# Experts stage: activations turned two chunks at a time, placing next to the turns of gathered rows, Silu on ScalarE

## The reference, cut to what matters

```python
def expert_block(args):
    xb, e = args
    u = xb @ w1[e] + b1[e]
    glu = jnp.minimum(u[:, ::2], SWIGLU_LIMIT)
    lin = jnp.clip(u[:, 1::2], -SWIGLU_LIMIT, SWIGLU_LIMIT)
    a = glu * jax.nn.sigmoid(SWIGLU_ALPHA * glu) * (lin + 1.0)
    return a @ w2[e] + b2[e]
```

## Time and profile before

| | us |
|---|---|
| median of the runs | 3635.84 |
| the profiled execution, device time | 3630.8 |
| its span, from the first to the last instruction | 3629.0 |
| units of experts, 790.5 to 2034.7 of the span | 1244 |

### The profile page before, as it was taken

One profiled execution on the slowest core, in us unless ns is written; L12 is line 12 of the kernel. 1 busy time (PEld: TensorE's weight loads), 2 busy tenths in 40 slices (PEclk: granted clock), 3 DMA queues, 4 the chain that ended last, 5 costly groups with the idle time before them and its releaser, 6 DMA issues. The chain is left out here.

```text
span 3629.0 us, 55793 instructions
## 1 busy us (share of the span) xinstructions
PE 3391.6 (93%) x20926; PEld 2738.5 (75%) x20926; DVE 2085.2 (57%) x2480; ACT 1764.9 (49%) x2318; POOL 1051.8 (29%) x435
## 2 busy tenths in 40 slices
PE   7989999989999999999999698899999987789997
PEld 4877777668888888888888584678887856678886
DVE  3320121279999999999999625521153155346665
ACT  3222333257777777777777524432243243133333
POOL 1324222212323232323232240144443300034443
PEclk9999999989999999999999899999999978899999
DMA  8213343359999999999999627123222300013221
GB/s 280 85 59 99 118 137 123 102 192 383 365 382 365 384 362 384 363 383 363 382 363 382 237 77 267 66 90 96 93 93 71 103 32 4 7 59 103 94 93 41
DMA packets 245253, 696.82 MB, mean 192 GB/s; under 512 B 17742, under 2 KB 149570, under 8 KB 186484
## 3 DMA queue, kind: packets, MB, share of 16 engines
q1 hardware_dynamic: 234932, 658.42, 48.9%
q0 software_dynamic: 9936, 36.18, 3.8%
q10 hardware_dynamic: 240, 0.12, 0.0%
HBM read 668.90 MB, written 30.23 MB: 193 GB/s over the span
## 5 line engine op out<-in xcount | busy, mean ns | idle before, releaser
L325 POOL TENSOR_TENSOR split_w<-ring,split_w 128x1024 fp32r<-128x1024 f32 (+1 forms) x294 | 698.2, 2375 | 1618.0 <-ACT split_w L320 1464.8
L2177 DVE TENSOR_TENSOR moe_low<-ring,moe_high 128x2048 fp32r<-128x2048 f32 x408 | 929.4, 2285 | 18.4 <-ACT moe_high L2167 17.4
L2167 ACT ACTIVATE moe_high<-ring 128x1024 fp32r<-128x1024 f32 x810 | 827.6, 1058 | 102.9 <-PE psum L2421 102.8
L320 ACT ACTIVATE split_w<-ring 128x1024 fp32r<-128x1024 f32 (+1 forms) x294 | 304.7, 1037 | 1030.6 <-PE psum L496 600.8
L2417 PE MATMUL psum<-moe_high,moe_xe 128*128 128x512 f32 x2176 | 585.6, 391 | 0.0
L2417 PEld LDWEIGHTS psum<-moe_high,moe_xe 128*128 128x128 f32 x2176 | 410.3, 189 | 83.6
L2328 POOL DMA_INDIRECT moe_y_rows<-moe_ye,moe_target x34 | 197.4, 5807 | 684.3 <-DVE moe_ye L2232 684.3
L496 PE MATMUL psum<-pair,split_w 128*128 128x512 f32 x1488 | 337.9, 389 | 0.0
L2421 PE MATMUL psum<-moe_low,moe_xe 128*128 128x512 f32 x1088 | 336.4, 391 | 0.0
L496 PE MATMUL psum<-b_pair,split_w 128*128 128x512 f32 x1392 | 321.8, 393 | 5.8 <-PEq L1406 2.6
L496 PEld LDWEIGHTS psum<-pair,split_w 128*128 128x128 f32 x1488 | 279.3, 188 | 58.7 <-issue 0.9
(11 more groups left out here) (640 smaller groups left out, 4342.7 us busy)
## 6 DMA issues: line engine op xcount, KB each, us to landing
ring<-in_w_experts SPq DMA_DIRECT2D x408, 1024.0 KB, 7.5
ring<-in_w_mod SPq DMA_DIRECT2D x48, 1024.0 KB, 6.7
ring<-in_w_in SPq DMA_DIRECT2D x39, 1024.0 KB, 5.2
ring<-in_w_up SPq DMA_DIRECT2D x33, 1024.0 KB, 5.1
ring<-in_w_in SPq DMA_DIRECT2D x44, 512.0 KB, 5.2
ring<-in_w_down SPq DMA_DIRECT2D x20, 1024.0 KB, 5.1
ring<-in_w_gate SPq DMA_DIRECT2D x11, 1024.0 KB, 5.3
ring<-in_w_out SPq DMA_DIRECT2D x8, 1024.0 KB, 6.5
```

Of the source, the lines that this page charges most:

```text
L320: self.nc.scalar.activation(high, raw, ACT.Copy).then_inc(self.K.rounded, 1)
L325: self.nc.gpsimd.tensor_tensor(low, raw, high.bitcast(F32), ALU.subtract).then_inc(self.K.split, 1)
L2167: self.nc.scalar.activation(self.B["high"][:, j % HALVES, :], self.raw(j), ACT.Copy).then_inc(self.high, 1)
L2177: self.nc.vector.tensor_tensor(flat(self.low_of(j, 2)), self.K.ring[:, self.ring_slot(j // 2), :], high, ALU.subtract).then_inc(self.low, 2)
```

## The change

Five things change, all in the experts' units.

- Activations are turned in two groups of four transposes instead of four groups of two. turn(0) takes chunks 0 and 1 and stands after half 9, in the middle of chunk 2; turn(1) takes chunks 2 and 3 and stands behind half 17. ScalarE's copy and VectorE's low part become two instructions of 128x512 each instead of four of 128x256.
- `pe_place` moves from behind chunk 0 to behind half 17, ahead of `pe_x_turn`, and works for the unit after the next. It also waits for `esel`, and a first placing stands before the loop.
- ScalarE computes Silu of 1.702 times the gate part instead of the sigmoid; one of VectorE's two multiplies per chunk (L2257) goes, and the factor 1/1.702 is put into the gates by one multiply of 128x1024 before the stage.
- The slots' base is subtracted by VectorE in `dve_stage` instead of being added by a matmul (L2388); two copies that prepared its operands go.
- On VectorE `dve_stage` moves ahead of low(8), `dve_pick` between clamp(1) and low(12), `dve_esel` between clamp(3) and multiply(3); on ScalarE the high parts are grouped anew around the gates and copies.

```diff
@@ class Experts, dve_unit @@
-        def low_of_turned(c):
-            ve.wait_ge(self.aT_high, u * 4 + (c + 1))
+        def low_of_turned(g):
+            ve.wait_ge(self.aT_high, u * 2 + (g + 1))
...
         def multiply(c):
-            ve.wait_ge(self.sig, u * 4 + (c + 1))
-            ve.wait_ge(self.clamped, u * 8 + (2 * c + 1))
-            nc.vector.scalar_tensor_tensor(B["glu"][:, c % 2, :], B["sig"][:, c % 2, :], SIG_LIMIT, B["lin"][:, c % 2, :],
-                                           ALU.min, ALU.mult).then_inc(self.clamped, 1)
-            ve.wait_ge(self.clamped, u * 8 + (2 * c + 2))
-            nc.vector.scalar_tensor_tensor(B["a"][:, c % 2, :], self.K.ps[:, c % 2, 0:256], LIMIT, B["glu"][:, c % 2, :],
+            ve.wait_ge(self.glu, u * 4 + (c + 1))
+            ve.wait_ge(self.clamped, u * 4 + (c + 1))
+            nc.vector.scalar_tensor_tensor(B["a"][:, c % 2, :], B["glu"][:, c % 2, :], GLU_LIMIT, B["lin"][:, c % 2, :],
                                            ALU.min, ALU.mult).then_inc(self.act_done, 1)
         low(6)
         clamp(0)
+        if ahead:
+            self.dve_stage(ve, u + 1)
         low(8)
         multiply(0)
-        if ahead:
-            self.dve_stage(ve, u + 1)
         low(10)
         clamp(1)
+        if ahead:
+            self.dve_pick(ve, u + 2)
         low(12)
         multiply(1)
+        low(14)
         low_of_turned(0)
-        low(14)
         clamp(2)
         low(16)
         multiply(2)
-        low_of_turned(1)
         low(18)
         clamp(3)
-        low(20)
-        multiply(3)
-        low_of_turned(2)
-        low(22)
         if ahead:
             self.dve_esel(ve, u + 1)
-        low_of_turned(3)
+        multiply(3)
+        low(20)
+        low_of_turned(1)
+        low(22)
         low(24)
...
@@ act_unit @@
-        nc.scalar.activation(B["unused"], self.K.ones[:, 0:1], ACT.Sigmoid)
+        nc.scalar.activation(B["unused"], self.K.ones[:, 0:1], ACT.Silu)
         high(6, 7, 8, 9)
-        sigmoid(0)
+        gate(0)
         high(10, 11, 12, 13)
-        sigmoid(1)
+        gate(1)
+        high(14, 15)
         turned(0)
-        high(14, 15, 16, 17)
-        sigmoid(2)
+        high(16, 17)
+        gate(2)
+        high(18, 19)
+        gate(3)
+        high(20, 21)
         turned(1)
-        high(18, 19, 20, 21)
-        sigmoid(3)
-        turned(2)
         high(22, 23, 24)
-        turned(3)
         if ahead:
             self.act_xe(sc, u + 1)
         high(25, 26, 27, 28, 29)
@@ pe_place, pe_unit @@
         if not first:
             pe.wait_ge(self.staged, v)
-        nc.tensor.matmul(out, B["eye"][:, :], B["slot_base"][:, :], start=True, stop=False)
+            pe.wait_ge(self.esel, v)
...
-        def turn(c):
-            pe.wait_ge(self.act_done, u * 4 + (c + 5))
-            pe.wait_ge(self.aT, u * 4 + (c + 4))
-            for i in range(2):
+        def turn(g):
+            pe.wait_ge(self.act_done, u * 4 + (2 * g + 6))
+            pe.wait_ge(self.aT, u * 2 + (g + 2))
+            for i in range(4):
...
             for i in range(4):
                 product(ps[:, c % 2, :], B["xe"], 4 * c + i, 2 * i, True)
-            if c:
-                turn(c - 1)
-            if c == 0 and ahead:
-                self.pe_place(pe, u + 1)
+                if (c, i) == (2, 1):
+                    turn(0)
...
             product(ps[:, 6 + m, :], B["aT"], j, 2 * k, False)
-            if j == 17 and ahead:
-                self.pe_x_turn(pe, u + 1)
-            if j == 18:
-                turn(3)
+            if j == 17:
+                if ahead:
+                    self.pe_place(pe, u + 2)
+                    self.pe_x_turn(pe, u + 1)
+                turn(1)
@@ mixture, TensorE before the loop @@
                 X.pe_x_turn(pe, 0)
+                X.pe_place(pe, 1)
                 pe.wait_ge(y_started, NT)
                 with pe.Fori(0, n1) as u:
                     X.pe_unit(pe, u)
```

More of the change, by code:

```diff
@@ L1924, in dve_step @@
             ve.wait_ge(self.b2_high, 1)
+            nc.vector.tensor_scalar(self.gates, self.gates, 1.0 / ALPHA, None, ALU.mult)
             nc.vector.tensor_tensor(self.b2[64:96, :], self.b2_raw[64:96, :], self.b2[64:96, :].bitcast(F32),
@@ L2129 @@
 LIMIT, ALPHA = 7.0, 1.702
-SIG_LIMIT = 1.0 / (1.0 + math.exp(-ALPHA * LIMIT))
+GLU_LIMIT = ALPHA * LIMIT / (1.0 + math.exp(-ALPHA * LIMIT))
 class Experts:
@@ L2143, in __init__ @@
         self.x_turned, self.xe_high, self.xe = n_("x_turned"), n_("xe_high"), n_("xe")
-        self.clamped, self.sig, self.act_done = n_("clamped"), n_("sig"), n_("act_done")
+        self.clamped, self.glu, self.act_done = n_("clamped"), n_("glu"), n_("act_done")
         self.kept, self.aimed, self.retired = n_("kept"), n_("aimed"), n_("retired")
@@ L2210, in dve_stage @@
             ve.wait_ge(self.kept, v)
-        nc.vector.tensor_scalar(B["source"][:, :], B["ps_place"][:, 0:1], -1.0, None, ALU.mult)
+        nc.vector.scalar_tensor_tensor(B["source"][:, :], B["ps_place"][:, 0:1], -1.0, B["slot_base"], ALU.mult,
+                                       ALU.subtract)
         nc.vector.tensor_reduce(B["gate_u"][:, bass.ds(v, 1)], B["ps_place"][:, 2:4], AX, ALU.add)\
@@ L2240, in low @@
             self.split(self.dve_low, ve, u, js, ahead)
-        def low_of_turned(c):
-            ve.wait_ge(self.aT_high, u * 4 + (c + 1))
-            out = B["aT"][:, :, 2 * c:2 * c + 2, :]
-            nc.vector.tensor_tensor(out[:, 1, :, :].rearrange("p a b -> p (a b)"), self.K.ps[:, 3, 0:256],
+        def low_of_turned(g):
+            ve.wait_ge(self.aT_high, u * 2 + (g + 1))
+            out = B["aT"][:, :, 4 * g:4 * g + 4, :]
+            nc.vector.tensor_tensor(out[:, 1, :, :].rearrange("p a b -> p (a b)"), self.K.ps[:, 3, :],
                                     out[:, 0, :, :].rearrange("p a b -> p (a b)").bitcast(F32), ALU.subtract)\
@@ L2293, in dve_unit @@
         self.dve_y(ve, u, 1)
-        if ahead:
-            self.dve_pick(ve, u + 2)
         low(28)
@@ L2349, in high, with gate, turned @@
             self.split(self.act_high, sc, u, js, ahead)
-        def sigmoid(c):
-            sc.wait_ge(self.clamped, u * 8 + (2 * c + 1))
+        def gate(c):
+            sc.wait_ge(self.clamped, u * 4 + (c + 1))
             sc.wait_ge(self.act_done, u * 4 + (c + 3))
[L2354 to L2360, removed]
-        nc.scalar.activation(B["unused"], self.K.ones[:, 0:1], ACT.Sigmoid)
+            nc.scalar.activation(B["glu"][:, c % 2, :], self.K.ps[:, c % 2, 0:256], ACT.Silu, scale=ALPHA)\
+                .then_inc(self.glu, 1)
+        def turned(g):
+            sc.wait_ge(self.a_turned, u * 2 + (g + 3))
+            nc.scalar.activation(B["aT"][:, 0, 4 * g:4 * g + 4, :].rearrange("p a b -> p (a b)"),
+                                 self.K.ps[:, 3, :], ACT.Copy).then_inc(self.aT_high, 1)
+        nc.scalar.activation(B["unused"], self.K.ones[:, 0:1], ACT.Silu)
         high(6, 7, 8, 9)
-        sigmoid(0)
+        gate(0)
         high(10, 11, 12, 13)
-        sigmoid(1)
+        gate(1)
+        high(14, 15)
         turned(0)
-        high(14, 15, 16, 17)
-        sigmoid(2)
+        high(16, 17)
[3 more added lines that the diff above has]
+        high(20, 21)
         turned(1)
-        high(18, 19, 20, 21)
-        sigmoid(3)
-        turned(2)
         high(22, 23, 24)
-        turned(3)
         if ahead:
@@ L2387, in pe_place @@
             pe.wait_ge(self.staged, v)
-        nc.tensor.matmul(out, B["eye"][:, :], B["slot_base"][:, :], start=True, stop=False)
+            pe.wait_ge(self.esel, v)
         for t in range(NT):
-            ins = nc.tensor.matmul(out, B["pick"][:, t, :], B["gcol"][:, t, :], start=False, stop=(t == NT - 1))
+            ins = nc.tensor.matmul(out, B["pick"][:, t, :], B["gcol"][:, t, :], start=(t == 0), stop=(t == NT - 1))
         ins.then_inc(self.placed, 1)
@@ L2438, in pe_unit @@
                 pe.wait_ge(self.y_ready, u * 2 + (m + 1))
-            if m == 0:
-                pe.wait_ge(self.aT, u * 4 + (k + 5))
+            if m == 0 and k % 2 == 0:
+                pe.wait_ge(self.aT, u * 2 + (k // 2 + 3))
             product(ps[:, 6 + m, :], B["aT"], j, 2 * k, False)
-            if j == 17 and ahead:
-                self.pe_x_turn(pe, u + 1)
-            if j == 18:
-                turn(3)
+            if j == 17:
[3 more added lines that the diff above has]
+                turn(1)
 def expert_source(A, e, chunk):
@@ L2469, in __init__ @@
              "h_rows": rows[0], "y_rows": rows[1], "iota": R.iota[:, :],
-             "sig": lane(4), "glu": lane(5), "lin": lane(6), "a": lane(7),
-             "b1": R.b1, "eye": R.eye, "slot_base": R.slot_base, "unused": R.slots[:, 7:8],
+             "glu": lane(5), "lin": lane(6), "a": lane(7),
+             "b1": R.b1, "slot_base": R.slots[:, 0:1], "unused": R.slots[:, 7:8],
              "gate_u": sb("gate_u", [P, EXPERTS + SPILLS + 1]), "gcol": R.gcol,
@@ L2544, in _ @@
```

(5 more changed lines are left out.)

5 lines of the change are left out of this document (1 added, 4 removed).

## The result

The changed kernel takes 3793.37 us, the median of four runs (3789.92 to 3795.84); the kernel before, beside it, 3635.78 us (3631.22 to 3636.49). The ratio is 1.043, with a 95% interval of 1.041 to 1.044: 158 us slower. The forecast was 3791.

What follows compares the result with a forecast made beforehand. The prediction took TensorE as the bound before, at 36.5 us a unit, and a loop of waits plus half clock after, at 41.0: 33 x (41.0 - 36.5) + 5.7 + 1 = 155 us on 3635.8 gives 3791, range 3728 to 3815.

Steps and rivals of the forecast that it cites:

- The bound and the gain: TensorE in each unit: 35.9 us if nothing waits, 0.6 less than before, 20 us over 33 units.
- Stretch (a): VectorE from the end of dve_xe_low to multiply(1), with 0.14 until TensorE starts: 17.0 us.
- Pause before turn(0): TensorE wants multiply(1) after half 9, before VectorE has it, and waits 2.5 us in each unit.
- (b): TensorE from the start of turn(0) to the end of turn(1): 13.4 us without the clock's cost.
- (c): From the end of turn(1) through ScalarE and VectorE to the end of dve_xe_low: 9.1 us; TensorE waits 1.0.
- The clock: Behind each turn(0), 3.4 us at half clock, costing 1.0 to 1.7 us a unit, taken as 1.5.
- clock holds: Rival in the units: the waits come as worked out but no half clock; 3742 us, chance 0.22.
- Start: Before unit 0, the first placing waits for dve_pick(1): beginning 5.7 us later, bounded by 3 and 6.
- Outside the stage: The multiply of the gates and two dropped copies, outside the units: between -0.4 and +1.2 us, taken as 0.
- The faster rival: In the units, multiply(1) comes before TensorE reaches turn(0), and TensorE's 35.9 us bounds: 3620 us, chance 0.06.

Runs made afterwards that it cites:

- e10: e7 with dve_stage moved behind multiply(0) on VectorE; 3619.6 us, ratio 0.996.
- e6: Changed kernel with all its parts, turn(0) still behind half 9, and new orders on VectorE and ScalarE; 3624.4 us, ratio 0.997.
- e8: Changed kernel with dve_pick behind multiply(1) instead of ahead of low(12); 3707.7 us.
- e4: Changed kernel with VectorE's order alone changed: multiply(1) directly behind clamp(1), low(12) and dve_pick later; 3661.6 us.
- e9: Changed kernel with the sigmoid and both multiplies back and the gates unscaled; 3809.0 us.
- e3: Changed kernel with ScalarE making high(22) and high(23) ahead of the copy turned(1); 3733.8 us.
- e7: Changed kernel with all its parts, turn(0) behind half 10, and other new orders on VectorE and ScalarE than e6; 3660.4 us.
- e2: Changed kernel with turn(0) one product later, behind half 10; 3691.8 us.

## Why the prediction was right

- **The bound and the gain.** TensorE's own work was worked out as 35.9 us a unit; the kernels without waits measured 35.98 and 36.02 (e10, e6). The gain was there, 0.5 us a unit; the order spent it. It was not the 20 us forecast, though: e6 and e10 lie 12 and 16 us under before, since they begin the stage 2 us later and their units gain 0.5, not 0.6.
- **Stretch (a), VectorE from the rows' low part to multiply(1).** 17.0 us worked out, 16.98 read off. That the pick's move doesn't count held: e8 takes it out of the stretch and gains its 0.86. That the stretch sets the unit is shown from both sides, by e4 (multiply earlier) and e9 (0.9 us longer, units without half clock 40.36 against 39.43 in the changed kernel's second unit).
- **Pause before turn(0).** 2.5 us worked out, 2.15 in the trace. Half of the difference is a matter of measure: the busy time of a matmul in the trace reaches beyond the start of the next one, 0.39 against steps of 0.23, and I had set the wait by the steps; by the steps it is 2.33. The rest is TensorE's way to turn(0), which took 14.65 us and not 14.5.
- **Stretch (b) and (c).** 13.4 + 1.5 for the clock against 14.87, and 9.1 against 9.11. ScalarE's copy ahead of the high parts cost 0.8 as a visible pause before the bias (1.0 was forecast, by the steps), and e3, which swaps them, gains 0.96.
- **The clock.** One stretch in each unit was taken, at 1.5 us; there were 31 in 33, at 1.54 (e3). The rival "clock holds" had 39.5 us a unit, and the changed kernel's second unit, which had no stretch, took 39.43. The Trainium skill (TensorE: Matmul & The Clock Gate, section HAM oscillation — how this bites in real kernels) warns of re-throttling only for idle gaps longer than these. By it the clock would have held; here gaps of 2.15 us were followed by half clock 31 times, and the measurement decides. But my own reading, that a pause of this length always brings it, was too simple as well. In e3 15 of 33 pauses of the same length brought it, in e9 not even all of 3.1 us. One of my readings was off, too: I called the pause before 3563 2.4 us, which is the length of the stretch in the earlier trace rows; the list of instructions has 2.76 us, ended at 3563.4, so "2.5 is more than either of the two pauses that cost" doesn't hold. And one trace could not have told the rule. The same pause in unchanged code behind the experts, 2.56 us before TensorE's L692, was followed by half clock in the profiled execution of before and not in that of the changed kernel (each time a row of the list of instructions, then one of the busy time by stretch, PEclk 0.50 and 1.00):

```profile
3502.25 7.97 PE L692 MATMUL psum<-split_w,b_hpair 128*128 128x512 f32 x28 [2.56 <-DVE b_hpair L573]
3502.20:3505.00 2.80, 2.75 (x7) 2.21 (x8) 2.77 (x2) 1.75 (x2) 1.92 (x1) 0.50 0.00 0
```

```profile
3664.85 10.33 PE L692 MATMUL psum<-split_w,b_hpair 128*128 128x512 f32 x43 [2.56 <-DVE b_hpair L573]
3664.80:3668.20 3.40, 3.35 (x15) 2.81 (x16) 3.37 (x2) 1.76 (x2) 2.42 (x1) 1.00 0.00 0
```

So part of the exactness of the forecast is luck: had every second unit gone without, as in e3, some 24 us would have been missing, still in the range.
- **Start.** 5.7 us later was worked out. With `dve_pick(1)` behind the low parts, from the end of the first low part of the gathered rows to the first bias the trace shows 0.14 us before and 6.20 after, so 6.1; with dve_pick(1) ahead of the first low parts (e6, e7, e10) it is 2.1.
- **Outside the stage.** Taken as nothing. In the two profiled executions the part behind the last unit took 1605 us after and 1595 before, with unchanged code. In the other kernels it was between 1598 and 1609, so I take that for the variation of an execution. The medians differ by 158; the later start and the longer stage together account for 152.

The faster rival needed stretch (a) under 14.5 us; it was 16.98. e4 is the kernel in which that rival's condition is fulfilled, and even there the waits at half 20 (0.3 us) and at the unit's start (0.2 us) remained, and the unit was 0.6 us longer than before. So the rival's condition was necessary, not sufficient.

## What to carry to other kernels

When every engine runs a fixed list, cost a reordering as a loop: pick one event that recurs in each round, follow it through the lists of all engines until it comes back, and add the steps. The loop is the period, whatever the busy shares say; here it gave 40.96 us to 0.1, with 1.5 us of it put in for the clock. A step that waits for two results at once (a turn of two chunks) must be placed by the later one, and the list of the engine that makes it has to be moved with it. And to a pause of two microseconds or more in a stream of matmuls add the price of a half-clock stretch, 1.3 to 1.6 us here, as a chance and not as a certainty, until the trace shows how often it comes.

## What the runs showed of the hardware that I had not expected

- The granted clock after a pause isn't settled by the length of the pause. Pauses of 2.1 to 2.2 us were followed by 3.4 us at 1.2 GHz in 31 of 33 units of the changed kernel and in 15 of 33 of e3; pauses of 3.1 us (e9) by nothing, by 3.4 us or by 6.8 us. Pauses of 0.8 and 1.3 us (e2, e8) were never followed by it. In the kernel before, behind the experts, one of 1.91 us (before 3241.4) was, with 3.4 us at 0.50 from 3242.3 on, and one of 1.80 us wasn't.
- In the changed kernel the stretch began 0.01 to 0.14 us ahead of the end of the pause in each unit from the third on, and the units repeated themselves to within 0.1 us. In e3, with units of 38.46 and 40.00 us, it came in about every second, 0.6 to 1.5 us behind the pause; in e9 it began between 0.8 us ahead of the pause's end and 0.5 us behind it. What decides it was not tried.
- An instruction's place can hide a wait for another engine: `dve_stage` waited for GpSimd's copy only where one low part less stood between the second `dve_y` and it (e7, 1.37 us); in the changed kernel the copy was done 0.2 us before VectorE asked for it.
